# Two norms that write x in its own order and by halves, and a gather that loads its weights with a stride

## What is computed

```python
def first_block(x, ...):
    for i in range(DEPTH):                                  # DEPTH = 2
        f = mla_mixer(x, ...) if i % 2 == 0 else pool_mixer(x, ...)
        x = layer_norm(DEEPNORM_ALPHA * x + f, ln_g[i, 0], ln_b[i, 0])
        f = hier_moe(x, moe_w_grp[i], ..., moe_w_exp[i], ..., moe_w1[i], moe_w3[i], moe_w2[i])
        x = layer_norm(DEEPNORM_ALPHA * x + f, ln_g[i, 1], ln_b[i, 1])
    return x
```

## Time and profile before

| what | value |
|---|---|
| median of 3 runs | 2062.06 us |
| the profiled execution: its time, its span | 2062.14 us, 2060.4 us |
| mean granted TensorE clock | 0.954 |
| busy: TensorE, VectorE, ScalarE, GpSimd | 88%, 40%, 19%, 6% of the span |
| chain that ended last: TensorE, DMA, VectorE, SyncE's queue | 57%, 28%, 7%, 5% |
| HBM read, over the span | 578.95 MB, 285 GB/s with what is written |
| expert loop of layer 0, of layer 1 (first to last up product) | 142 to 586 us, 654 to 1098 us |
| norm 0 with its route, norm 2 with its route | 97 to 142 us, 617 to 654 us |

### The profile page before, as it was taken

One profiled execution on the slowest core, in us unless ns is written; L12 is line 12 of the kernel. 1 busy time (PEld: TensorE's weight loads), 2 busy tenths in 40 slices (PEclk: granted clock), 3 DMA queues, 4 the chain that ended last, 5 costly groups with the idle time before them and its releaser, 6 DMA issues.

```text
span 2060.4 us, 34718 instructions
## 1 busy us (share of the span) xinstructions
PE 1803.1 (88%) x14736; PEld 1152.4 (56%) x14736; DVE 819.2 (40%) x1340; ACT 389.0 (19%) x892; POOL 133.5 (6%) x188
## 2 busy tenths in 40 slices
PE   8998776677699877766869999999999999999998
PEld 5665555555557655554554448746554458746553
DVE  6541111111144111111115753473657753473656
ACT  4521011011112100100112122222221122222221
POOL 3100000000000000000001401100221001100000
PEclk9999898899899998889889999999999999999999
DMA  9799999999999999999998674443546374443331
GB/s 353 217 379 420 420 420 421 420 420 420 420 392 388 419 420 421 420 420 420 420 420 318 163 244 156 135 163 123 173 154 213 100 246 154 135 163 123 133 123 62
DMA packets 182598, 593.84 MB, mean 288 GB/s; under 512 B 51236, under 2 KB 52644, under 8 KB 133544
## 3 DMA queue, kind: packets, MB, share of 16 engines
q1 hardware_dynamic: 173896, 572.70, 71.3%
q0 software_dynamic: 8544, 18.89, 3.7%
HBM read 578.95 MB, written 8.39 MB: 285 GB/s over the span
## 4 chain that ended last, share of the span: by engine, by line
PE 57%; DMA 28%; DVE 7%; SPq 5%; issue 2%; ACT 1%; DVEq 0%; ACTq 0%
DMA ring<-in_moe_w_dram 28%; PE ps L651 20%; PE ps L618 9%; PE ps L1686 5%; PE ps L624 3%; SPq L1397 2%; PE ps L1721 2%; PE ps L1668 2%; PE ps L595 1%; PE ps L533 1%; PE ps L1963 1%; PE ps L628 1%; SPq L506 1%; SPq L1406 1%; PE ps L1741 1%
## 5 line engine op out<-in xcount | busy, mean ns | idle before, releaser
L1686 PE MATMUL ps<-ring,xT 128*32 128x128 f32 x8192 | 303.2, 306 | 178.0 <-DMA ring<-in_moe_w_dram 170.9
L1686 PEld LDWEIGHTS ps<-ring,xT 128*32 128x32 f32 x8192 | 262.5, 121 | 244.4 <-DMA ring<-in_moe_w_dram 185.3
L2383 DVE TENSOR_TENSOR arena<-arena,ps 128x256 f32<-128x256 f32 x32 | 13.5, 421 | 561.5 <-ACT arena L2057 561.5
L618 PE MATMUL ps<-xT,ring 128*128 128x256 f32 x896 | 199.2, 380 | 0.9 <-DMA ring<-in_w_in_dram 0.9
L651 PE MATMUL ps<-ring,xT 128*128 128x512 f32 x432 | 194.2, 594 | 0.5 <-ACT xT L785 0.5
L1092 DVE TENSOR_TENSOR ring<-ring 128x2048 f32<-128x2048 f32 x80 | 183.4, 2292 | 20.0 <-PE ps L651 5.9
L618 PEld LDWEIGHTS ps<-xT,ring 128*128 128x128 f32 x896 | 168.0, 190 | 26.7 <-issue 3.3
L1721 PE MATMUL ps<-arena 128*32 128x512 f32 x768 | 120.0, 606 | 31.6 <-DVE arena L2383 31.6
L1330 POOL DMA_DIRECT2D ring<-gap_bias x160 | 96.1, 643 | 786.7 <-DMA ring<-in_w_in_dram 475.5
L1668 PE MATMUL ps<-arena,x_tm 128*128 128x128 f32 x1024 | 137.6, 291 | 0.9 <-issue 0.9
L1668 PEld LDWEIGHTS ps<-arena,x_tm 128*128 128x128 f32 x1024 | 129.1, 205 | 11.6 <-issue 11.6
(11 more groups left out here) (315 smaller groups left out, 2027.4 us busy)
## 6 DMA issues: line engine op xcount, KB each, us to landing
ring<-in_moe_w_dram SPq DMA_DIRECT2D x287, 1024.0 KB, 26.1
ring<-in_w_in_dram SPq DMA_DIRECT2D x52, 2048.0 KB, 9.3
arena<-in_moe_w_dram SPq DMA_DIRECT2D x89, 1024.0 KB, 26.7
ring<-in_w_br_diff_dram SPq DMA_DIRECT2D x4, 2048.0 KB, 10.5
ring<-in_w_out_dram SPq DMA_DIRECT2D x4, 2048.0 KB, 7.9
arena<-in_moe_w_dram SPq DMA_DIRECT2D x14, 512.0 KB, 14.7
ring<-in_w_mem_kv_dram SPq DMA_DIRECT2D x3, 2048.0 KB, 16.3
ring<-in_mla_w_o_dram SPq DMA_DIRECT2D x1, 4096.0 KB, 25.0
```

The source lines that it names most:

```text
L618: m = nc.tensor.matmul(bank[:, u * T:(u + 1) * T], w[:, k, f * P:(f + 1) * P], xT[:, k, :], start=(k == 0), stop=(k == KD - 1))
L1686: m = nc.tensor.matmul(ps[SL * q:SL * q + SL, g % 2, s * P:(s + 1) * P], xs[:, g % 2, k, s * SL:(s + 1) * SL], w[:, c0:c0 + 2 * P - 1:2], ...
```

## The change

- `layer_norm`, n = 0 and 2: the last instruction (L2290, one 128x1024, permuted) becomes two of 128x512 in x's own order, each followed by an increment of a new semaphore `ln_half`.
- `transpose_x`: for n > 0 it reads plain columns, and waits for `ln_half` before each four transposes; the waits on `ln_part` in front of it go.
- `pe_logits`: waits for each of the two copies before the four products that need it.
- The router weights are loaded by `(k p)` instead of `(p k)`, to fit the plain order.
- `gather`: the weights are `x_tm[:, t, k::KD]`, 128 words that lie 8 words (32 bytes) apart.
- ScalarE's `acc = ALPHA * x` reads and writes plain.
- The centred x of n = 0, t = 0 goes into `psc_raw` in place of `xT`, with a wait for GpSimd's scaling; `pool_scaled` and `memT_scaled` become one semaphore `scaled`.

```diff
@@ load_route
-            ...wr_of[layer][:, :, 0:NG], a["moe_w_grp"][layer].rearrange("(p k) n -> p k n", k=KD)
+            ...wr_of[layer][:, :, 0:NG], a["moe_w_grp"][layer].rearrange("(k p) n -> p k n", p=P)
...
@@ transpose_x
             for c in range(2):
+                if n:
+                    pe.wait_ge(sem("ln_half"), 4 * (n - 1) + 2 * t + c + 1)
                 for j in range(4):
                     k = 4 * c + j
                     i = nc.tensor.transpose(ps[:, 4 + 2 * t + c, j * P:(j + 1) * P],
-                                            x_kp[:, t, k, :] if n else x_tm[:, t, k::KD], ident)
+                                            x_tm[:, t, k * P:(k + 1) * P] if n else x_tm[:, t, k::KD], ident)
@@ gather
-                        m = nc.tensor.matmul(ps[:, 3 + half, (k % 4) * P:(k % 4 + 1) * P], x_kp[:, t, k, :],
+                        m = nc.tensor.matmul(ps[:, 3 + half, (k % 4) * P:(k % 4 + 1) * P], x_tm[:, t, k::KD],
@@ pe_logits
-            pe.wait_ge(sem("xT_ready"), 4 * (layer + 1) + 2 * t + 2)
             for k in range(KD):
+                if k % 4 == 0:
+                    pe.wait_ge(sem("xT_ready"), 4 * (layer + 1) + 2 * t + k // 4 + 1)
@@ block.tensor, four places
-            pe.wait_ge(sem("ln_part"), ...)
             transpose_x(pe, ...)
@@ act_x
-            nc.scalar.mul(acc[:, t, :].rearrange("p (q k) -> p q k", k=KD), x_qk[:, t], ALPHA).then_inc(
+            nc.scalar.mul(acc[:, t, :], x_tm[:, t, :], ALPHA).then_inc(
@@ layer_norm
-                centred = xT.rearrange("p k t -> p (k t)")[:, 0:D] if n == t == 0 else acc[:, t, :]
+                if n == t == 0:
+                    v.wait_ge(sem("scaled"), 4)
+                centred = psc_raw if n == t == 0 else acc[:, t, :]
...
-                    by_k = [b.rearrange("p (q k) -> p k q", k=KD) for b in (centred, s_)]
-                    ch(nc.vector.scalar_tensor_tensor(x_kp[:, t], by_k[0], agg[:, t, 1:2], by_k[1], ALU.mult, ALU.add))
+                    for half in (slice(0, 512), slice(512, D)):
+                        ch(nc.vector.scalar_tensor_tensor(x_tm[:, t, half], centred[:, half], agg[:, t, 1:2], s_[:, half],
+                                                          ALU.mult, ALU.add))
+                        v.sem_inc(sem("ln_half"), 1)
```

More of the change, by code:

```diff
@@ L293, in build @@
         pool_y = carve(arena, 0, TT, D)
-        x_kp = x_tm.rearrange("p t (k q) -> p t k q", k=KD)
-        x_qk = x_tm.rearrange("p t (k q) -> p t q k", k=KD)
         goh_e = tiny_at(TT, 8)
@@ L1416, in load_route @@
             got = sem("win_wr1_in" if layer else "route_in")
-            sp.dma_start(wr_of[layer][:, :, 0:NG], a["moe_w_grp"][layer].rearrange("(p k) n -> p k n", k=KD)).then_inc(
+            sp.dma_start(wr_of[layer][:, :, 0:NG], a["moe_w_grp"][layer].rearrange("(k p) n -> p k n", p=P)).then_inc(
                 got, 16)
-            sp.dma_start(wr_of[layer][:, :, NG:], a["moe_w_exp"][layer].rearrange("(p k) n -> p k n", k=KD)).then_inc(
+            sp.dma_start(wr_of[layer][:, :, NG:], a["moe_w_exp"][layer].rearrange("(k p) n -> p k n", p=P)).then_inc(
                 got, 16)
@@ L1940, in _ @@
             scores(1)
-            pe.wait_ge(sem("memT_scaled"), 1)
+            pe.wait_ge(sem("scaled"), 1)
             for h in range(NH + 1):
@@ L1966, in _ @@
                     if (t, n) == (1, 0):
-                        pe.wait_ge(sem("ln_part"), 1)
                         transpose_x(pe, 1, 0)
@@ L1970, in _ @@
             mem_values0(pe, 0, 6)
-            pe.wait_ge(sem("ln_part"), 2)
             pe.wait_ge(sem("mkv_taken"), 2)
@@ L2009, in _ @@
             mem_keys(pe, 1, 1, 7, 0, 10)
-            pe.wait_ge(sem("ln_part"), 5)
             transpose_x(pe, 2, 0)
@@ L2015, in _ @@
             mem_values(pe, 1, 0, 5, 0, 1)
-            pe.wait_ge(sem("ln_part"), 6)
             pe.wait_ge(sem("mkv_taken"), 6)
@@ L2574, in _ @@
             pool.wait_ge(sem("memT_taken"), 4)
[L2575 to L2578, removed]
+            nc.gpsimd.tensor_tensor(memT_of[0], memT, over(gm[:, 0, :], 2, T), ALU.mult).then_inc(sem("scaled"), 1)
+            pool.wait_ge(sem("scaled"), 1)
+            nc.gpsimd.tensor_tensor(memT, memT, over(gm[:, 1, :], 2, T), ALU.mult).then_inc(sem("scaled"), 1)
+            pool.wait_ge(sem("scaled"), 2)
             pool.dma_start(memT_dram.rearrange("p (k t) -> p k t", k=KD), memT).then_inc(sem("memT_out"), 16)
@@ L2586, in _ @@
             nc.gpsimd.tensor_tensor(by_group, by_group, over(psc_raw.rearrange("p (g n) -> p g n", n=PG), 2, 2),
-                                    ALU.mult).then_inc(sem("pool_scaled"), 1)
-            nc.gpsimd.tensor_tensor(pb_raw, pb_raw, psc_raw, ALU.mult).then_inc(sem("pool_scaled"), 1)
-            pool.wait_ge(sem("pool_scaled"), 2)
+                                    ALU.mult).then_inc(sem("scaled"), 1)
+            nc.gpsimd.tensor_tensor(pb_raw, pb_raw, psc_raw, ALU.mult).then_inc(sem("scaled"), 1)
+            pool.wait_ge(sem("scaled"), 4)
             pool.dma_start(pw_dram.rearrange("p (k n) -> p k n", k=KD), pw_raw).then_inc(sem("gap_pool_out"), 16)
```

## The result

Four runs of the changed kernel gave a median of 2080.19 us (2076.16 to 2084.95), beside 2062.03 us for the kernel before (four runs, 2061.0 to 2062.37). The ratio is 1.0084, 95% interval 1.0069 to 1.0098: about 18 us more. The profiled execution is the longest of the four, with a span of 2083.2 us; it is 22.8 us longer than the profile before, so what is read from it is some 4.6 us more than the medians show.

What follows compares the result with a forecast made beforehand. Full DMA was taken to bound both expert loops, TensorE and VectorE the stretches before them, where time won is kept. 2062.14 - 0.92 - 0.13 = 2061.09, so 2061.1 us; 8-in-10 range 2058.8 to 2064.2 us.

Steps and rivals of the forecast that it cites:

- The norm's write: VectorE's last norm instruction: halves ready after 0.75 and 1.65 us in place of 2.083, so a norm ends 0.43 us earlier.
- Norm 2, 0.92 us: Second tile of norm 2: TensorE's transposes start 0.92 us earlier, and the restart of weight loads moves with them.
- norm 0, 0.13 us: Norm 0: small gaps before TensorE's transposes and logits, read from the starts of matmuls, give 0.13 us.
- ScalarE's `acc`: Norm 2, first tile: plain `acc` gets 0.4 us or more shorter, so the second tile's square root adds no wait; 0.
- The added wait: First tile's centring in norm 0 now waits for GpSimd's scaling, which ends 9 us before; cost 0.
- the router weights: Router weight loads in the new layout: as many packets, landing before the projection begins; cost 0.
- the disputed cost, taken as 0: The gather: 1024 records load words 32 bytes apart, claimed to cost nothing over plain loads.
- I take 0, since the L1872 rows have the same stride, size and type: Gather: strided transposes load 0.112 us apart, the plain gather's pace, so the stride was taken to add 0.
- Rival 3: Gather: the strided load costs a 53 ns surcharge, 3.4 us over the two first gathers, 2064.5 us; chance 0.07.
- rival 4: Gather: strided loads take twice their pace, 7.2 us over the two first gathers, 2068.3 us; chance 0.08.
- The 15 later ones lie under full DMA: Gathers after each layer's first: off the path, as TensorE waits 5.4 us a group for expert weights; 0.
- the forecast's 1.05 us: Whole gain forecast at the norms: 0.92 us at norm 2 and 0.13 us at norm 0.

Runs made afterwards that it cites:

- plain_gather: The changed kernel with the gather's weights read plainly, so of other features; 2063.76 us, ratio 1.0003 to the kernel before.
- strided_middle: The kernel before with the gather read at a stride of 8 words only in gathers g = 1 to 14 of each loop; 2068.35 us, ratio 1.0020.
- strided_last: The kernel before with the gather read at a stride of 8 words only in each loop's last gather, g = 15; 2073.16 us, ratio 1.0044.
- strided_first: The kernel before with the gather read at a stride of 8 words only in each loop's first gather, g = 0; 2067.24 us, ratio 1.0021.
- strided_gather_only: The kernel before with all gather weights read at a stride of 8 words and nothing else changed; 2080.77 us, ratio 1.0081.

## Why the prediction was wrong

**The norm's write: right.** The pair takes 1.65 us, as worked out:

```profile
642.38 1.65 DVE L2289 SCALAR_TENSOR_TENSOR x_tm<-arena,tiny 128x512 f32<-128x512 f32 x2
```

**Norm 2, 0.92 us, and norm 0, 0.13 us: right.** 1.03 us and 0.14 us in the changed kernel, 1.03 and 0.13 in `plain_gather`. TensorE does not wait for VectorE there. Between the start of the value product in front of the transposes and that of the logits it is the 0.92 us to the hundredth (3.55 us before, 2.63 us now); the other 0.10 us is at the logits (1.84 us before, 1.74 us now).

**ScalarE's `acc`: right.** It fell from 2.03 us to 1.07 us, and the second tile's root was done at 640.68 us, before the end of its centring at 641.37 us:

```profile
639.52 1.07 ACT L2118 ACTIVATE arena<-x_tm 128x1024 f32<-128x1024 f32 x1
640.48 0.20 ACT L2104 ACTIVATE tiny<-tiny 128x1 f32<-128x1 f32 x1
```

With 0.96 us more for `acc` the root would have ended at some 641.6 us, 0.2 us after VectorE wants it (an estimate from these rows; no run has plain halves with the old `acc`).

**The added wait and the router weights: 0, right.** The scaling on GpSimd ended at 95.72 + 2.34 = 98.1 us, the centring started at 107.13 us. The stretch of norm 0 holds both, and it is shorter.

**The gather, "the disputed cost, taken as 0": wrong, and here the prediction fell.** Two steps of it failed.

The first is the sentence "I take 0, since the L1872 rows have the same stride, size and type". A strided transpose and a strided matmul load look alike in stride, size and type, and a plain matmul load has the length of a strided transpose load (192 and 193 ns). I read from this that the matmul's load is already at the slow pace and can't be slowed. In fact the slow pace of a matmul load is 0.24 us. The trace had the sign that the two kinds are not one: plain, they differ (140 and 192 ns), so a stride need not do to one what it does to the other. Rival 3's 53 ns on top of 192 ns give 245 ns a load; measured is 335 ns. Only rival 4, twice the pace, had the price about right (0.224 us; measured 0.243). I gave it 0.08, and let a row of another kind of instruction outweigh the rule that I had cited from the Trainium skill ("Advanced Engine Details and Errata", section "Memory Cachelines").

The second is "The 15 later ones lie under full DMA", which rival 4 used as well: with nearly the right pace it gave 2068.3 us. Its 7.2 us for the two first gathers were too much (4.3 us measured), and its 0 for all others too little. For the gathers from g = 2 to g = 14 the sentence was right: in `strided_middle` the DMA engines are full from 190 to 560 us. It failed at the two ends:
- At the tail: the DMA windows averaged 420 GB/s up to 576 us, and I took this for the loop. But the queue works ahead. The last wait for a weight ends at 556.86 us, 40 us before the loop does; behind it the chain has TensorE with short steps of ScalarE and VectorE, and the gather of g = 15 stands there. It costs 9.1 us in both layers together (`strided_last`): 3.5 and 4.0 us in the gather itself, and 1.7 us more in the down products behind it where they got the lower clock, for which the sum had no term.
- At the head, second gather: DMA is full, but full because TensorE frees slots in time. The cover was not the 5.4 us a group that TensorE waits on average; it was the backlog issued before the first release of a down slot. A gather of g = 1 that is 4.0 us late outlasts it, and some 2 us of the 4 come out at the end of each loop (`strided_middle`, 4.1 us for both).
- At the head, first gather: I had put it on the path in full in the rivals, and it is not. It delays TensorE by 3.9 us in each layer, the up loads that wait for the first up products come later, and 1.5 and 2.4 us of that are left at the ends of the loops (`strided_first`, 4.3 us for both).

So the forecast's 1.05 us were there in the stretches of the norms, and against them stood the gather's loss, 16.7 us by the ratio of `strided_gather_only` and 17.8 us by its medians.

## What to carry to other kernels

The cost of a strided stationary operand (the 128x128 weights that a matmul loads) is to be read from a strided operand of the same kind of instruction. If the trace has none, a look-alike is no bound: here the pace was 2.2 times the plain one. The slow load was free under a matmul of 512 columns and not under one of 128. In a loop bound by DMA, find where the last wait for data ends and where the first slots of each kind are released: of work added in front of the first releases half to two thirds was paid for here, of work behind the last wait all of it and something of the clock besides, however full the windows in between.

## What the runs showed of the hardware that I had not expected

- A 128x128 fp32 weight load of a matmul runs at 0.112 us when words are adjacent, 0.118 us with every second word, 0.239 us with every fourth and 0.243 us with every eighth. A transpose's loads with every eighth word run at 0.112 us, with adjacent words at 0.104 us. Why the two kinds differ, no run here shows.
- Under a 128x512 matmul the slow load (314 ns) is hidden but for 0.01 us a record.
- Behind a gather with a stride of 4 or 8 words and an idle stretch of 1.5 us, the granted clock of the next products fell in seven of eight cases (5.1 us in place of 3.4); behind a gather at 0.112 or 0.118 us a record and the same idle stretch in none of 18.
- VectorE's permuting pass costs more in two pieces than in one: 2.44 us against 2.08. (Word by word of this pass it is the two reads that go 8 words apart, while `x_kp` is written in its own order; that both jump holds only counted by feature.)
- Loads from HBM in runs of 1 KB for two thirds of the bytes moved 368 GB/s where runs of 8 KB moved 420.
